# A compressed attention branch's hidden layer: from split blocks in rows of products to unsplit blocks in four column groups of the array

## The reference, cut to what matters

```python
def compress(raw, pos, w1, w2):
    blocks = raw[:, :, idx] + pos                       # (1, 2, 15, 32, 64)
    return jax.nn.silu(blocks.reshape(B, G, n_cmp, 2048) @ w1) @ w2
k_cmp = compress(kc_raw, pos_k, w1_k, w2_k)             # w1: 2048 x 256, w2: 256 x 64
v_cmp = compress(vc_raw, pos_v, w1_v, w2_v)
```

## Time and profile before

| | |
|---|---|
| median of three runs | 931.54 us (930.29 to 932.63) |
| time of the profiled execution | 931.82 us |
| its span in the trace | 930.0 us |
| PE busy | 897.2 us, 96% of the span |
| DVE, ACT, POOL busy | 584.8, 490.4, 113.4 us |
| mean granted clock of PE | 0.996 |

### The profile page before, as it was taken

The page is one execution under the profiler, slowest core; times in us unless marked ns, Lnnn a source line. Parts: engine busy times, 40 slices in busy tenths (PEclk is TensorE's granted clock), DMA queues, the critical chain, the costliest instruction groups (busy, mean ns, idle before and its releaser), DMA issues.

```text
span 930.0 us, 14231 instructions
## 1 busy us (share of the span) xinstructions
PE 897.2 (96%) x4869; PEld 760.7 (82%) x4869; DVE 584.8 (63%) x879; ACT 490.4 (53%) x732; POOL 113.4 (12%) x107
## 2 busy tenths in 40 slices
PE   6999999999899999999999999998999999999986
PEld 5788888888787887888888878787888999999875
DVE  5655555558865456655555558989676667667664
ACT  6544444456755646544444457565646445445463
POOL 5120000020044302000000022631002000000020
PEclk9999999999999999999999999999999999999999
DMA  9796766538722334665565527342165555655511
GB/s 315 214 273 192 220 197 196 166 118 271 233 85 92 95 108 146 208 192 183 184 196 187 192 75 253 131 136 92 46 203 192 181 189 172 200 184 180 182 46 46
DMA packets 122040, 157.43 MB, mean 169 GB/s; under 512 B 10047, under 2 KB 83011, under 8 KB 122000
## 3 DMA queue, kind: packets, MB, share of 16 engines
q1 hardware_dynamic: 119648, 151.65, 51.0%
q0 software_dynamic: 1904, 4.65, 1.9%
q10 hardware_dynamic: 448, 0.59, 0.2%
HBM read 155.79 MB, written 1.07 MB: 169 GB/s over the span
## 4 chain that ended last, share of the span: by engine, by line
PE 83%; DVE 8%; ACT 4%; issue 2%; SPq 1%; DMA 1%; DVEq 0%; ACTq 0%
PE bank L475 21%; PE bank L477 21%; PE bank L476 20%; PE bank L505 4%; PE bank L507 4%; PE bank L506 4%; DVE w_lo L1733 2%; ACT w_hi L1212 1%; PE bank L587 1%; PE bank L859 1%; PE bank L688 1%; PE bank L869 1%; DMA w_raw<-in_w_ffn_up 1%; SPq L382 1%; ACT junk L1235 1%
## 5 line engine op out<-in xcount | busy, mean ns | idle before, releaser
L1740 DVE TENSOR_TENSOR w_lo<-w_raw,w_hi 128x1024 fp32r<-128x1024 f32 x180 | 220.2, 1224 | 177.3 <-ACT w_hi L1221 177.3
L1221 ACT ACTIVATE w_hi<-w_raw 128x1024 fp32r<-128x1024 f32 x180 | 190.3, 1058 | 210.4 <-PE bank L477 173.7
L475 PE MATMUL bank<-w_hi,x_hi 128*128 128x512 f32 (+1 forms) x680 | 273.5, 402 | 7.4 <-DVE hb L1771 2.4
L477 PE MATMUL bank<-w_hi,x_lo 128*128 128x512 f32 (+1 forms) x680 | 265.4, 390 | 0.0
L476 PE MATMUL bank<-w_lo,x_hi 128*128 128x512 f32 (+1 forms) x680 | 264.7, 389 | 0.0
L475 PEld LDWEIGHTS bank<-w_hi,x_hi 128*128 128x128 f32 x680 | 128.5, 189 | 37.4 <-issue 6.4
L1733 DVE TENSOR_TENSOR w_lo<-w_raw,w_hi 128x1024 fp32r<-128x1024 f32 x97 | 121.2, 1277 | 50.2 <-ACT w_hi L1212 49.7
L477 PEld LDWEIGHTS bank<-w_hi,x_lo 128*128 128x128 f32 x680 | 128.3, 189 | 27.5
L476 PEld LDWEIGHTS bank<-w_lo,x_hi 128*128 128x128 f32 x680 | 128.7, 189 | 23.8 <-issue 0.2
L1212 ACT ACTIVATE w_hi<-w_raw 128x1024 fp32r<-128x1024 f32 x108 | 111.8, 1054 | 56.1 <-PE bank L477 53.7
L475 PE MATMUL bank<-w_hi,h_hi 128*128 128x512 f32 (+1 forms) x312 | 119.6, 383 | 5.7 <-DVE h_lo L1882 2.5
(11 more groups left out here) (299 smaller groups left out, 881.9 us busy)
## 6 DMA issues: line engine op xcount, KB each, us to landing
w_raw<-in_w_ffn_gate SPq DMA_DIRECT2D x132, 256.0 KB, 2.9
w_raw<-in_w_ffn_up SPq DMA_DIRECT2D x132, 256.0 KB, 3.1
w_raw<-in_w_ffn_down SPq DMA_DIRECT2D x132, 256.0 KB, 3.0
w_raw<-in_w_in SPq DMA_DIRECT2D x104, 256.0 KB, 3.0
w_raw<-in_w_out SPq DMA_DIRECT2D x32, 256.0 KB, 3.3
w_raw<-in_w_ple_gate SPq DMA_DIRECT2D x16, 256.0 KB, 3.4
arena<-bias_rows POOLq DMA_DIRECT2D x8, 256.0 KB, 4.8
w_raw<-in_cmp_w_k SPq DMA_DIRECT2D x8, 256.0 KB, 4.5
```

Of the source, the lines that this page charges most:

```text
L475: pe.matmul(out_, hi, wh, start=start, stop=False)
L477: return pe.matmul(out_, lo, wh, start=False, stop=stop)
L1221: act.activation(whi[:, slot * UNIT:(slot + 1) * UNIT], raw[:, slot * UNIT:(slot + 1) * UNIT], ACT.Copy).then_inc(sem("hi_done"), 1)
L1740: dve.tensor_tensor(wlo[:, s_], raw[:, s_], whi[:, s_].bitcast(F32), ALU.subtract).then_inc(sem("lo_done"), 1)
```

## The change

The blocks `Z` and the weights w1 are no longer split: the hidden layer takes plain fp32 operands, `Z` and `raw`. Its 16 steps of k are spread over four groups of 32 columns of the array, so that step kk of each unit writes partitions 32 kk to 32 kk + 31 of the bank, and each group sums four steps. `Z` has 32 columns a step in place of 30, with two zero columns. ACT copies the four partial sums to `HIDB` (now 128 partitions), and `hid_turn` is a plain fp32 product of `HIDB` with a constant 128 x 30 (four identities below one another), which sums the four groups and turns the result at once. Silu comes after it, on the turned result, on ACT.

The eight units of w1 are `WHOLE`: no `split` on ACT or DVE. SP may overwrite their slots only when PE has used them (`room`). Unit `U_QA[1]` moves in front of the units of `U_CV` in the ring. The fillers before the values' hidden layer become four in place of two, one stands between the two `hid_turn`s, and `FILL_AT` has 19 places in place of 22. `hid_turn` leaves the loop for the place before it.

```diff
...
 U_CK = U_QB + 4
-U_CV = U_CK + 5
-U_QA = (U_CK + 4, U_CV + 4, U_CV + 5, U_CV + 6)
+U_CV = U_CK + 6
+U_QA = (U_CK + 4, U_CK + 5, U_CV + 4, U_CV + 5)
 U_KA = U_QA[3] + 1
+WHOLE = tuple(range(U_CK, U_CK + 4)) + tuple(range(U_CV, U_CV + 4))
 U_VA = U_KA + 4
...
 C_FREQ = C_HEAD + 8
-C_ALL = C_FREQ + 8
+C_GROUP = C_FREQ + 8
+C_ALL = C_GROUP + 2 * N_CMP
...
         c[h * N_CMP:(h + 1) * N_CMP, C_HEAD + h] = 1.0
+    for g in range(4):
+        c[32 * g:32 * g + 2 * N_CMP, C_GROUP:C_GROUP + 2 * N_CMP] = np.eye(2 * N_CMP)
     c[:, C_FREQ:C_FREQ + 8] = np.float32(500000.0) ** (-np.arange(8, dtype=np.float32) / np.float32(8))
...
         PT = a1.take(2 * REV)
-        Z = a1.take(2 * 480)
+        Z = a1.take(2 * 512)
         HIDK = a1.take(60)
...
-        PL0, PL1 = U_QA[1] + RING, U_OUT1 + 6
+        PL0, PL1 = U_KA + 3, U_OUT1 + 6
+        def whole(u):
+            return sum(w < u for w in WHOLE)
...
                 return sem("lo_pool"), u - PL0
-            return sem("lo_done"), u if u <= PL0 else u - (PL1 - PL0)
+            return sem("lo_done"), u - whole(u) - (0 if u <= PL0 else PL1 - PL0)
         def lo_shift(base):
-            return PL1 - PL0 if base >= PL1 else 0
-        FILL_AT = (0, 1, 2, 3, 4, 4, 5, 6, 7, 8, 9, 9, 10, 11, 12, 13, 14, 14, 15, 16, 16, 17)
+            return PL1 - PL0 + len(WHOLE) if base >= PL1 else 0
+        FILL_AT = tuple(range(18)) + (4,)
         OUT_AT = ((0, 0, 18), (0, 1, 19), (1, 0, 20), (1, 1, 21), (3, 0, 22), (4, 0, 23), (2, 0, 24), (2, 1, 24))
...
+                if u - RING in WHOLE:
+                    sp.wait_ge(sem("w_used"), u - RING + 1)
+                    return
                 sp.wait_ge(*lo_ready(u - RING + 1))
...
                     load_qa(0)
+                    load_qa(1)
                 w1 = t[name][0].rearrange("(k p) n -> p k n", p=P)
...
                                      w1[:, 4 * j + 2 * b:4 * j + 2 * b + 2, :]).then_inc(sem(f"landed{slot}"), 16)
-            for j in range(1, 4):
+            for j in range(2, 4):
                 load_qa(j)
...
-            for s_, base in ((0, U_CK), (1, U_CV)):
-                pe.wait_ge(sem("z_done"), s_ + 1)
+            def hid_units(s_, base):
+                pe.wait_ge(sem("zf_done"), 2 * (s_ + 1))
                 for j in range(4):
                     u = base + j
-                    pe.wait_ge(*lo_ready(u + 1))
+                    pe.wait_ge(sem(f"landed{u % RING}"), 32 * (u // RING + 1))
                     for kk in range(4):
-                        k = 4 * j + kk
                         c = (u % RING) * UNIT + kk * 256
-                        zs = slice(k * 30, k * 30 + 30)
-                        last = three(bank[4 + s_][0:30, 0:256], hhi[:, zs], hlo[:, zs],
-                                     whi[:, c:c + 256], wlo[:, c:c + 256], k == 0, k == 15)
+                        last = pe.matmul(bank[4 + s_][32 * kk:32 * kk + 32, 0:256], av(Z + 512 * s_ + 32 * (4 * j + kk), [32]),
+                                         raw[:, c:c + 256], start=(j == 0), stop=(j == 3))
                     last.then_inc(sem("w_used"), 1)
-                if s_ == 0:
-                    filler()
-                    filler()
-                    tgroup(4, stg_tile)
-                    tgroup(5, lambda m, q: stg_tile(m, 2 + q))
             def hid_turn(s_):
                 pe.wait_ge(sem("hid_done"), s_ + 1)
+                pe.wait_ge(sem("con2_in"), 16)
                 pe.wait_ge(sem("tg_done"), 6)
                 for ht in range(2):
-                    mm = pe.transpose(bank[2 + s_][:, ht * 30:ht * 30 + 30],
-                                      av(HIDB + 256 * s_ + ht * P, [P], 0, 30), ident[0:30, 0:30])
+                    mm = pe.matmul(bank[2 + s_][:, ht * 30:ht * 30 + 30], av(HIDB + 256 * s_ + ht * P, [P]),
+                                   con[:, C_GROUP:C_GROUP + 30], start=True, stop=True)
                 mm.then_inc(sem("hidt_full"), 1)
+            hid_units(0, U_CK)
+            for _ in range(4):
+                filler()
+            tgroup(4, stg_tile)
+            tgroup(5, lambda m, q: stg_tile(m, 2 + q))
+            hid_units(1, U_CV)
+            hid_turn(0)
+            filler()
+            hid_turn(1)
...
-                if s_ == 1:
-                    hid_turn(0)
-                    hid_turn(1)
                 if s_ == 2:
...
-                if v >= UNITS:
+                if v >= UNITS or v in WHOLE:
                     return
...
                     split(u + j + RING)
-                    if p == 2 and j == 2:
-                        act.wait_ge(sem("zf_done"), 2)
-                        act.activation(hhi[:, 0:480], av(Z, [480]), ACT.Copy).then_inc(sem("zhi_done"), 1)
                 staged(p, u + 4)
...
-            for s_, u in ((0, U_CK), (1, U_CV)):
-                for j in range(4):
-                    split(u + j + RING)
-                if s_ == 0:
-                    act.wait_ge(sem("zf_done"), 4)
-                    act.wait_ge(sem("w_used"), U_CK + 4)
-                    act.activation(hhi[:, 0:480], av(Z + 480, [480]), ACT.Copy).then_inc(sem("zhi_done"), 1)
-                    filler()
-                    filler()
+            def hid_sums(s_, u):
                 act.wait_ge(sem("w_used"), u + 4)
-                act.activation(av(HIDB + 256 * s_, [256], 0, 30), bank[4 + s_][0:30, 0:256], ACT.Silu
-                               ).then_inc(sem("hid_done"), 1)
+                act.activation(av(HIDB + 256 * s_, [256]), bank[4 + s_][:, 0:256], ACT.Copy).then_inc(sem("hid_done"), 1)
+            hid_sums(0, U_CK)
+            for _ in range(4):
+                filler()
+            hid_sums(1, U_CV)
+            act.wait_ge(sem("hidt_full"), 1)
+            act.activation(av(HIDK, [60]), bank[2][:, 0:60], ACT.Silu).then_inc(sem("hidk_done"), 1)
+            split(U_CV + RING)
+            act.wait_ge(sem("hidt_full"), 2)
+            for ht in range(2):
+                act.activation(av(HIDV + 120 * ht, [2, 4, N_CMP]),
+                               raw_ap(bank[3], 512, 30 * ht, [[N_CMP, 2], [0, 4], [1, N_CMP]]),
+                               ACT.Silu).then_inc(sem("hidv_done"), 1)
+            split(U_CV + 1 + RING)
             act.wait_ge(sem("gates_raw"), 2)
             act.activation(sm(GATES, 48), sm(GATES, 48), ACT.Sigmoid).then_inc(sem("gates_done"), 1)
+            for j in (2, 3):
+                split(U_CV + j + RING)
+            filler()
             small_exps()
...
             def beside(s_):
-                if s_ == 2:
-                    act.wait_ge(sem("hidt_full"), 2)
-                    for ht in range(2):
-                        act.activation(av(HIDV + 120 * ht, [2, 4, N_CMP]),
-                                       raw_ap(bank[3], 512, 30 * ht, [[N_CMP, 2], [0, 4], [1, N_CMP]]),
-                                       ACT.Copy).then_inc(sem("hidv_done"), 1)
                 if s_ == 6:
...
-                if v >= UNITS:
+                if v >= UNITS or v in WHOLE:
                     return
                 s_ = slice((v % RING) * UNIT, (v % RING + 1) * UNIT)
-                dve.wait_ge(sem("hi_done"), v + 1)
+                dve.wait_ge(sem("hi_done"), v + 1 - whole(v))
                 dve.tensor_tensor(wlo[:, s_], raw[:, s_], whi[:, s_].bitcast(F32), ALU.subtract
...
                 s_ = slice((v0 % RING) * UNIT, (v0 % RING + 1) * UNIT)
-                dve.wait_ge(sem("hi_done"), i * 6 + (v0 + 1))
+                dve.wait_ge(sem("hi_done"), i * 6 + (v0 + 1 - whole(base)))
                 dve.tensor_tensor(wlo[:, s_], raw[:, s_], whi[:, s_].bitcast(F32), ALU.subtract
...
                 src = (KC, VC)[s_]
+                dve.memset(raw_ap(arena, ARENA, Z + 512 * s_ + 30, [[32, 16], [1, 2]]), 0.0)
                 for e in range(2):
...
                     i1 = raw_ap(cols_a, ROWS_A, R_POS + 16 * s_, [[1, 16], [0, 2], [0, N_CMP]], 64 * e, 64)
-                    dve.tensor_tensor(av(Z + 480 * s_, [16, 2, N_CMP], 64 * e, 64), i0, i1, ALU.add
-                                      ).then_inc(sem("zf_done"), 1)
-            def z_lo(s_):
-                dve.wait_ge(sem("zhi_done"), s_ + 1)
-                dve.tensor_tensor(hlo[:, 0:480], av(Z + 480 * s_, [480]), hhi[:, 0:480].bitcast(F32), ALU.subtract
-                                  ).then_inc(sem("z_done"), 1)
+                    o = raw_ap(arena, ARENA, Z + 512 * s_, [[32, 16], [N_CMP, 2], [1, N_CMP]], 64 * e, 64)
+                    dve.tensor_tensor(o, i0, i1, ALU.add).then_inc(sem("zf_done"), 1)
...
                 p, u, j, m = fill.pop(0)
-                if u == U_QA[0] and m:
+                if u in U_QA[0:2] and m:
                     split(u + RING)
...
             tg(2)
-            z_lo(0)
             tg(3)
...
             small_values()
-            for j in range(4):
-                split(U_CK + j + RING)
-            z_lo(1)
-            filler()
-            filler()
+            for _ in range(4):
```

(9 more changed lines are left out.)

## The result

The changed kernel takes 934.96 us, the median of 13 runs (932.78 to 936.07); the kernel before, run beside it 13 times, 932.01 us (930.29 to 933.26). The medians differ by 2.95 us, 0.32%. The ratio over all runs is 1.0025 (95% interval 1.0018 to 1.0033), which is 2.3 us. So the changed kernel is slower, by about the 0.3% or 2.8 us that the prediction called the least that a measurement of this kernel can tell. The forecast was 932.9, its range 926.5 to 937. The profiled execution of the changed kernel took 933.64 us, its span is 931.9; its time belongs to the lower of two bunches into which the 13 runs fall (932.8 to 933.6, and 935.0 to 936.1).

A forecast was written before the change was run, and what follows sets the result against it. PE, busy 96% of the span, was taken as the bound. Of 9.9 us saved on PE, late loads and queues left 0.3; clock falls cost 1.7: +1.4, 932.9 us as a median, range 926.5 to 937.

The forecast's parts named there:

- A side of the hidden layer, 2.0 us: On PE, four column groups overlap fully, as scores' row groups do: 2.0 us a side, bounds 2.0 and 6.9.
- New wait ahead of the first filler, 1.4: On PE, the first filler waits for staged(2) on DVE, behind z(1), until 236.8: a new wait of 1.4 us.
- `U_QA[3]` lands at about 246.0: Slots free only after PE's use, so six units load at once from 234.0; U_QA[3] lands at about 246.0.
- Rival A: Late loads are hidden: U_QA[3] lands at 243.2, everything 2.8 us earlier, no clock fall: 928.4 us; chance 0.22.
- `hid_turn(0)` at 249.6 after 4.3 us: After the values' layer PE idles 4.3 us, to 249.6, for DVE's copies behind splits of late units.
- First exp at 259.5, `scores(2)` at 258.4 after 2.6: ACT's queue puts exp(0) at 259.5; scores(2) on PE waits 2.6 us for DVE's ttr(0), to 258.4.
- A wait of 1.1 us for `staged(5)`: In the loop, the filler of step 3 waits another 1.1 us for staged(5) on DVE, behind ttr(3).
- The clock, two falls, 1.7 us: PE's clock falls after each of two idle times, half covered by ACT waits: 1.7 us, between 0 and 3.4.
- Rival C: The clock stays down: two falls fully on PE's work plus the loop's bound, +4.5 us, 936.0; chance 0.13.
- The whole: Whole kernel: -0.3 + 1.7 = +1.4 us on the profiled execution's 931.8, so 933.2; 932.9 as a median.
- The forecast's case: Case D: short layer, late loads, two long waits and clock falls: 929 to 935 us; chance 0.45.
- rival B: Column groups don't overlap in fp32: 6.9 us a side on PE, +3.8 us, 935.3, slower; chance 0.2.

The follow-up runs named there:

- run 1: Changed kernel with all 16 products of a hidden-layer side sent to one column group, hid_turn on 32 partitions: 937.55 us, ratio 1.0060 to the kernel before.
- run 2: Changed kernel with DVE's copies tg(4) and tg(5) ahead of the four fillers' splits: 930.99 us, ratio 0.9990 to the kernel before.
- run 3: Changed kernel loading only the first half of each of the four U_CV units, result not the reference's: 930.2 us, ratio 0.9977 to the kernel before.
- run 4: Changed kernel plus throwaway PE products, twelve ahead of hid_turn(0) and six ahead of scores(2): 932.48 us, ratio 1.0004 to the kernel before.
- run 5: Changed kernel with Sigmoid and small exps moved earlier on ACT, behind hid_sums(0): 932.59 us, ratio 1.0003 to the kernel before.
- 6 both orders: Changed kernel with the edits of run 2 and run 5 together: 930.6 us, ratio 0.9985 to the kernel before.
- 7 later splits: 6 both orders, with three splits moved from before the loop into its steps 1 to 5 on ACT and DVE: 926.36 us, ratio 0.9945 to the kernel before.
- run 8: 7 later splits, with staged(2) and the split of U_QA[1] ahead of z(1) on DVE: 926.83 us, ratio 0.9957 to the kernel before.
- run 9: Changed kernel, own orders, with ACT copying each w1 unit to free SBUF so its slot frees early: 928.26 us, ratio 0.9961 to the kernel before.
- run 10: Early loads by ACT copies as in run 9, with the orders of run 8: 926.66 us, ratio 0.9939 to the kernel before.
- run 11: Early loads by ACT copies as in run 9, with the orders of 7 later splits: 926.60 us, ratio 0.9942 to the kernel before.

## Why the prediction was right, point by point

**The sum can be checked in all runs.** PE sets the pace of this stage, so its length should be that of before, less what the change takes from PE, plus the new waits, plus 1.7 us for each 3.41 us at the low clock (half of them, as 0.50 is granted). The change takes 11.1 - 2 x 1.93 = 7.2 in the layers, 3.3 in waits, and adds 0.5: 10.0 us. New waits are all those of PE from 200 to 350 us that the kernel before doesn't have.

| | new waits | low clock, us x 0.5 | reckoned | stage measured, against before |
|---|---|---|---|---|
| after | 7.5 | 3.4 | +0.9 | +0.8 |
| 1 one group (layers 14.2) | 2.6 | 1.7 | +4.6 | +4.9 |
| 2 copies first | 6.0 | 1.7 | -2.3 | -2.1 |
| 3 half loads | 6.3 | 3.4 | -0.3 | -0.4 |
| 4 gaps filled (4.1 more work) | 5.2 | 0 | -0.7 | +0.1 |
| 5 ACT's queue | 7.4 | 5.1 | +2.5 | +2.4 |
| 6 both orders | 5.7 | 1.7 | -2.6 | -2.2 |
| 7 later splits | 4.1 | 0 | -5.9 | -5.3 |
| 8 staged first | 2.3 | 3.4 | -4.3 | -4.3 |
| 9 early loads | 5.2 | 1.7 | -3.1 | -3.0 |
| 10 early, orders of 8 | 3.1 | 0 | -6.9 | -6.1 |
| 11 early, orders of 7 | 4.5 | 0 | -5.5 | -4.7 |

All within 0.8 us, but the gaps have a pattern: the four runs without a fall of the clock lie 0.6 to 0.8 above what is reckoned, the others closer. With 9.4 us in place of 10.0 for what the change takes, and 1.4 in place of 1.7 for each 3.41 us at the low clock, a fit to these twelve rows, all come out within 0.25 us; and run 4 had shown 1.3 a fall by itself. Which of the terms behind the 10.0 is 0.6 too large, no run shows. So some 9.4 us were there, and in the changed kernel three waits (7.5) and two falls (2.6 to 2.8) ate them.

- *A side of the hidden layer, 2.0 us.* 1.93. The choice between 2.0 and 6.9 by the row of `scores` was right; run 1 shows the other end.
- *New wait ahead of the first filler, 1.4.* 1.62.
- *`U_QA[3]` lands at about 246.0.* ACT's wait for it ends at 246.03; run 3 shows that bytes decide, run 9 that the time of the issue does. Rival A, which had it landed by 243.2, was false. Run 9 comes near it by making the loads early: A had -3.1 us on the kernel before, run 9's stage is -3.0. That the two agree so well is luck, as run 9 has other waits and still one fall.
- *`hid_turn(0)` at 249.6 after 4.3 us.* 249.69 after 3.95. Run 2 shows the cause in DVE's order.
- *First exp at 259.5, `scores(2)` at 258.4 after 2.6.* 260.42; 259.43 after 1.90, both 1 us later than I wrote, as PE ran at a clock of 0.50 from 250.9 to 254.3. I had listed ACT's queue rightly. What I had not seen is that its order matters more than its length (runs 6 and 7).
- *A wait of 1.1 us for `staged(5)`.* Not in the changed kernel, but 1.1 us in run 4 and 1.2 in run 10, where the clock doesn't fall.
- *The clock, two falls, 1.7 us.* Two falls, where forecast. No run shows the 1.7 by itself: the traces show 3.41 us at a granted clock of 0.50 a fall, and by run 4 the two cost 2.6. The waits came out about 2 us shorter than forecast (3.95 for 4.3, 1.90 for 2.6, none for 1.1): products at the low clock fill time that would else be waited. I had counted this cover with the clock, the trace shows it in the waits. Together I forecast +1.4 for the stage, and it is +0.8, from misses that partly cancel: waits 2 us too long, falls 0.9 too cheap, and 0.5 too much taken from PE. That an idle time of over 2 us ends in a fall was no safe step either: the trace before has 2.06 us of idle time with a clock of 0.66 behind it, but also 2.54 us near 884 us with the clock at 1.00 behind it (last section). Rival C had the falls at their full 3.4, but with a loop 1.4 us longer for fillers that come out of step, of which no row shows anything.
- *The whole.* Forecast +1.4 us; the profiled executions differ by +1.8, the medians by +2.95. That +1.8 is so near +1.4 is partly luck: 0.8 of it is the stage, and 1.0 lies outside it, where I had put nothing. The profiled execution is of the lower bunch, and where the upper bunch loses its 2 us more is open. The record's mean granted clock is 0.990 to 0.992 in the six lower runs and 0.986 to 0.990 in the seven upper ones, so more time at the low clock goes with it, by the size of one or two falls; whether in the stage or outside, no trace shows.

The forecast's case was the right one, with its mechanism: the short layer, the late loads, both long waits with their releasers and both falls came as described. Its blind side was that I took the loss as given by the change, but over 5 us of it hung on the place of a few splits in two queues. The forecast was also low: 934.96 lies inside the range, but 2.1 us above 932.9 and above 934.3, in the part to which I had given 0.32. It is nearest to rival B's 935.3, whose mechanism the 1.93 us of a side rule out: by the median alone one would have picked the wrong story.

## What to carry to other kernels

When work is taken from the engine that sets the pace, look at what was hidden beside it: here a buffer's slot came free at the consumer's end in place of a copy's, the loads behind it bunched, and work that waits for a landing stood in two in-order queues ahead of work that was ready. Put what waits for late transfers behind what is ready, on each engine, or free the slot by a copy on an idle engine; either gave back gain here (stage -5.3 and -3.0 us against the kernel before). Together they are not a sum: -4.7 in run 11, and -6.1 only with `staged(2)` moved as well (run 10). And check a wait's cause one step further than its name: the wait of PE for DVE's copy was one for a DMA.

## What the runs showed that I had not expected

**The same idle time is followed by a fall of the clock in one run and not in the other**, and a fall costs up to 1.6 us far from the edit. Runs 10 and 11 near 643 us: the time line of PE and two windows of each, run 10 first.

```profile
643.11 0.55 PE L488 MATMUL bank<-w_hi,x_hi 128*128 128x512 f32 x1 [2.06 <-DVE arena L2328]
```

```profile
640.00:645.00 5.00, 2.94 (x15) 2.43 (x14) 3.85 (x7) 3.51 (x10) 0.00 (x0) 0.84 0.31 107
645.00:650.00 5.00, 5.00 (x30) 4.40 (x30) 1.09 (x1) 1.06 (x1) 0.00 (x0) 0.82 0.32 105
```

```profile
644.13 0.50 PE L488 MATMUL bank<-w_hi,x_hi 128*128 128x512 f32 x1 [2.06 <-DVE arena L2328]
```

```profile
640.00:645.00 5.00, 2.94 (x22) 2.59 (x21) 4.66 (x9) 4.43 (x12) 0.00 (x0) 1.00 0.34 119
645.00:650.00 5.00, 5.00 (x37) 4.63 (x36) 1.44 (x2) 1.06 (x1) 0.00 (x0) 1.00 0.32 107
```

The wait is the same, 2.06 us, and the code is the same. The part from the table load near 357 us to the one near 717 took 359.3 to 359.4 us in the five profiled executions with this fall (before, after, runs 2, 4 and 10), and 357.7 to 357.8 in the eight without. The same holds near 885 us, the time line of PE before and then after:

```profile
884.31 0.47 PE L475 MATMUL bank<-w_hi,h_hi 128*128 128x512 f32 x1 [2.54 <-DVE h_lo L1882]
```

```profile
885.48 0.52 PE L486 MATMUL bank<-w_hi,h_hi 128*128 128x512 f32 x1 [2.54 <-DVE h_lo L1894]
```

The first is followed by a clock of 1.00, the second by 0.66 in its window of 5 us, and the last part took 187.24 and 187.91 us. In all 13 profiled executions it took 187.24 to 187.25 us in the three without this fall (before, runs 1 and 11) and 187.88 to 188.10 in the ten with it. That is the +0.67 of the first section: no work of the change, but a fall; why it comes in one execution and not in another, no run here shows. So between versions of this kernel some 2 us of a difference can come from these two falls, and a difference of that size needs the stage's own length, not the median, to be put down to an edit.

**A fall isn't always as short.** The last 12 us of the kernel left aside, 3.41 us at a clock of 0.50 is what most falls in these traces show, but 6.83 us stood behind 2.32 us of waiting (run 8) and 10.24 behind 4.92 (run 5).
